# Expert weights in one kernel of a hybrid decoder step: down weights as 8 KB pieces, gate and up products by even and odd columns

## The reference

```python
def swiglu(x, w_g, w_u, w_d):
    return (jax.nn.silu(x @ w_g) * (x @ w_u)) @ w_d

# moe_ffn: each token picks 8 of 64 experts (4 of 8 groups first)
def body(y, inp):
    e, toks, wr = inp
    out = swiglu(x[toks], w_gate[e], w_up[e], w_down[e]) * wr[:, None]
    return y.at[toks].add(out), None
```

## Time and profile before

| what | value |
|---|---|
| time, median of 3 runs | 1742.17 us (1738.51 to 1746.92) |
| the profiled execution's own time | 1733.91 us |
| its span | 1732.1 us |
| TensorE busy (matmul) | 1619.7 us, 94% |
| VectorE, ScalarE, GpSimd busy | 708.6, 441.4, 146.3 us |
| moved by DMA | 552.38 MB, 319 GB/s over the span |

### The profile page before, as it was taken

The page is one execution under the profiler, slowest core; times in us unless marked ns, Lnnn a source line. Parts: engine busy times, 40 slices in busy tenths (PEclk is TensorE's granted clock), DMA queues, the critical chain, the costliest instruction groups (busy, mean ns, idle before and its releaser), DMA issues. The chain is left out here.

```text
span 1732.1 us, 30697 instructions
## 1 busy us (share of the span) xinstructions
PE 1619.7 (94%) x11617; PEld 968.6 (56%) x11744; DVE 708.6 (41%) x1912; ACT 441.4 (25%) x993; POOL 146.3 (8%) x206
## 2 busy tenths in 40 slices
PE   5999898899999999999998998889999999999997
PEld 4677575555555555555466766665555555555554
DVE  3133427263333333333336944165733333333334
ACT  2210113122222222222232124132222222222223
POOL 0000300000000000000020024000000000000000
PEclk9899789899999999999999969999999999999999
DMA  9875534999999999999682533546999999999990
GB/s 364 342 267 177 206 122 165 364 382 402 416 414 417 416 412 413 415 416 412 246 304 74 195 118 116 201 176 271 391 408 417 415 416 415 414 415 416 413 384 27
DMA packets 139032, 552.38 MB, mean 319 GB/s; under 512 B 19407, under 2 KB 36637, under 8 KB 104662
## 3 DMA queue, kind: packets, MB, share of 16 engines
q1 hardware_dynamic: 120562, 513.82, 74.8%
q0 software_dynamic: 15392, 34.66, 5.7%
q10 hardware_dynamic: 3012, 3.00, 0.6%
HBM read 562.74 MB, written 8.60 MB: 330 GB/s over the span
## 5 line engine op out<-in xcount | busy, mean ns | idle before, releaser
L1370 PE MATMUL PS<-ring,arena 128*64 128x256 f32 x4288 | 492.4, 383 | 2.5 <-ACT arena L1689 1.5
L1370 PEld LDWEIGHTS PS<-ring,arena 128*64 128x64 f32 x4288 | 305.1, 138 | 183.5 <-issue 40.0
L1394 PE MATMUL PS<-ring,arena 128*64 128x512 f32 x1072 | 259.6, 605 | 1.4 <-ACT arena L1674 1.4
L1596 DVE TENSOR_TENSOR arena<-arena,PS 128x128 f32<-128x128 f32 x134 | 38.6, 288 | 375.8 <-ACT arena L1672 369.9
L1333 PE MATMUL PS<-arena 128*128 128x512 bf16 x669 | 169.4, 384 | 15.4 <-issue 9.2
L1580 DVE TENSOR_SCALAR arena<-arena 128x512 bf16<-128x512 f32 x130 | 62.8, 483 | 256.5 <-ACT arena L1683 256.5
L1682 ACT COPY arena<-PS 64x512 f32<-64x512 f32 x134 | 77.5, 578 | 302.2 <-PE PS L1394 302.2
L1394 PEld LDWEIGHTS PS<-ring,arena 128*64 128x64 f32 x1072 | 65.0, 136 | 120.4 <-issue 104.1
L1333 PEld LDWEIGHTS PS<-arena 128*128 128x128 bf16 (+1 forms) x796 | 69.6, 99 | 91.9 <-issue 27.7
L1672 ACT ACTIVATE arena<-PS 128x128 f32<-128x128 f32 x134 | 37.2, 278 | 328.1 <-PE PS L1370 328.1
L1324 PEld LDWEIGHTS PS<-cst,arena 128*128 128x128 f32 x552 | 72.0, 194 | 80.2 <-issue 78.3
(11 more groups left out here) (504 smaller groups left out, 1584.3 us busy)
## 6 DMA issues: line engine op xcount, KB each, us to landing
ring<-in_moe_w_gate SPq DMA_DIRECT2D x134, 1024.0 KB, 8.7
ring<-in_moe_w_up SPq DMA_DIRECT2D x134, 1024.0 KB, 11.0
ring<-in_moe_w_down SPq DMA_DIRECT2D x134, 1024.0 KB, 15.4
ring<-in_w_ada SPq DMA_DIRECT2D x32, 1152.0 KB, 10.9
ring<-in_w_ada SPq DMA_DIRECT2D x16, 768.0 KB, 13.8
ring<-in_gla_w_in SPq DMA_DIRECT2D x8, 1152.0 KB, 12.6
ring<-in_dsa_w_in SPq DMA_DIRECT2D x6, 1024.0 KB, 19.2
arena<-in_state_gla POOLq DMA_DIRECT2D x8, 512.0 KB, 5.9
```

Of the source, the lines that this page charges most:

```text
L1370: m = pe.matmul(PS[64 * half:64 * half + 64, 5, 0:256].rearrange("p (g n) -> p g n", g=2), rows[:, k, CAP * b:CAP * b + CAP], gu[:, :, k, ...
L1394: m = pe.matmul(PS[64 * j:64 * j + 64, 7, :], hTt[b][:, kk * CAP:(kk + 1) * CAP], ring[:, s, 2, kk * D + 512 * j:kk * D + 512 * j + 512], ...
```

## The change

Partition p gets the rows 2p and 2p + 1 of an expert's down matrix, which are neighbours, so a partition's share is one piece of 8 KB. The two halves of the hidden columns are then no longer 0 to 127 and 128 to 255, but the even and the odd ones, so that the turned `hm` has entry 2p in its first half and 2p + 1 in its second. The gate and up product takes them by a step of two floats in its streamed operand. The shared expert's weights (`sp_moe`) are not touched.

```diff
--- before.py
+++ after.py
@@ -1136,13 +1136,11 @@
             return [wg.rearrange("(p k) n -> p (k n)", k=KT), wu.rearrange("(p k) n -> p (k n)", k=KT),
-                    wd.rearrange("(k p) n -> p k n", p=P)]
+                    wd.rearrange("(p k) n -> p (k n)", k=2)]
 
         def load_expert(s, e, l, sem):
             for t, src in enumerate(expert_w(l, e)):
                 dst = ring[:, s, t, :]
-                if t == 2:
-                    dst = dst.rearrange("p (k n) -> p k n", k=2)
                 sp.dma_start(dst, src).then_inc(sem, 16)
 
@@ -1368,7 +1366,7 @@
                     m = pe.matmul(PS[64 * half:64 * half + 64, 5, 0:256].rearrange("p (g n) -> p g n", g=2), rows[:, k, CAP * b:CAP * b + CAP],
-                                  gu[:, :, k, half * P:(half + 1) * P], start=(k == 0), stop=(k == KT - 1), skip_group_check=True)
+                                  gu[:, :, k, half:2 * P:2], start=(k == 0), stop=(k == KT - 1), skip_group_check=True)
```

## The result

The changed kernel takes 1762.61 us (median; 1756.98 to 1764.04), the kernel before 1744.55 us. The ratio is 1.0122, 95% interval 1.0097 to 1.0146: slower by about 1.2%, 18 us. The forecast was no change.

The account below looks back on a forecast made before the run. The prediction took TensorE to pace the expert loops, with loads hidden. 1733.9 us profiled + 0 for loads + 0 for the product = 1733.9 us, or 1742 us for the median; range 1726 to 1808 us.

Parts of the forecast that it names:

- TensorE sets the pace: In the two expert loops TensorE was taken as the limit, busy 97.4%, with an expert taking 7.87 us.
- The loads are hidden: Expert weight loads land before use, 3.2 us in hand late in the first loop; cheaper down loads contribute 0 us.
- the creep of the landing time: In the first loop the down load's landing time rises by 2.5 us from the middle to the end.
- The price of a piece: Each DMA packet costs 15 ns beyond its bytes, so larger down pieces save 0.12 us an expert, hidden beside TensorE.
- The sign that was to go with it: In the changed kernel the down load was to land 2.5 us behind the up load, not 5.
- The step of two floats costs 0: In the gate and up product, the streamed operand's step of 8 bytes was taken to add 0 us.
- The reading that led to 0: From L1324's weight loads, 0.83 ns a fetch; two floats a fetch give 0.41 ns a column, as now, cost 0.
- The other reading, from L1977: For the gate and up product, 1.06 ns a fetch gives 0.53 against 0.41 ns a column: 31 ns a pass, 132 us.
- The rule that the prediction cites: SBUF reads keep full bandwidth with two hits per 16-byte line; a step of 8 bytes has two, so 0 us.
- rival B: The strided gate and up stream is slower: a partial price gives 26 to 66 us (1768 to 1808); chance 0.28.
- half-fetch price: In the gate and up product a fetch yields two useful floats, costing 31 ns a pass, 132 us.
- rival C: Loads are the loops' hidden pace, so the change is faster: 1726 us, or at most 1715; chance 0.11.

Follow-up runs that it names:

- short_4k: Kernel before with the gate and up product cut from eight to five contraction slices, down weights in 4 KB pieces: 1724.49 us, ratio 0.9976, with 136 expert bodies.
- short_8k: Kernel before with the same cut to five slices, down weights in 8 KB pieces and neighbouring columns: 1715.68 us, ratio 0.9926, with 136 expert bodies.
- pieces_2k: Kernel before with the down weights as four pieces of 2 KB a partition: 1746.73 us against 1740.15, ratio 1.0037.
- stride_only: Kernel before with only the gate and up product's step of two floats, down weights still in 4 KB pieces: 1760.99 us against 1740.15, ratio 1.0111.
- forms: Kernel before with 19 groups of passes added at its end, read in the profile only: steps of 1, 2, 3, 4 floats take 108, 113, 171, 227 ns a pass.
- other_slice: Changed kernel with the odd half taking contraction slices four ahead, so both streams read different 16-byte lines: 1762.51 us, ratio 1.0127.
- forms2: Kernel before with 13 more groups at its end (pairs, quads, eights, bfloat16), profile only: quads take 3.45 us a group filling lines, 3.64 us across lines.

## Why the prediction was wrong

- **TensorE sets the pace: right.** The edit on TensorE's passes alone gave 1.0111, the whole change 1.0122, the loads alone (in layer 1) 0.9998.
- **The loads are hidden: right, closer than thought.** The kernel before loads an expert in 7.92 us (119.19 MB in 300 us) and uses one in 7.865; the creep of the landing time fits this 0.7%, and the four slots of the ring carry it through 64 experts. The price of a piece was read as 15 ns and measured as 9 (short_4k against short_8k) and as 10 (pieces_2k: 8.06 - 7.895 us over 16 pieces). The term's contribution, 0, holds. The sign that was to go with it, a down load that lands 2.5 us behind the up load, came true (10.3 against 8.3 us), but it tells little: stride_only shows 11.2 against 8.9 us with 4 KB pieces.
- **The step of two floats costs 0: the step that failed.** The prediction laid a price of 0 and one of 31 ns a pass side by side and took 0. It was 5.2 ns. The reading that led to 0 has two faults. It took L1324's weight loads, 0.83 ns for a float on a line of its own, as the price of a line for a streamed operand; the forms show 1.77 ns for that. (0.83 ns need not be the price of a line at all: the loads of ordinary products with neighbours, L2462 and L2503 in forms, take 137 ns for 64 columns and 190 for 128, and that is 0.83 ns a column too.) And it set half of 0.83 against 0.41 ns a column, which is the spacing of two passes at once; one stream takes 0.84 ns a column. Two floats a line take 1.77/2 = 0.885 ns a column, against this 0.84. The other reading, from L1977, had the right form, half a line's price against a column's, but a line there costs 2.1 ns, not 1.77, and since the cost is a small difference of two near numbers, this made 31 ns out of 5. Why a line costs more in L1977 is open; no form had its step of 512 bytes.
- **The rule that the prediction cites.** The Trainium skill ("SBUF — State Buffer", in the note on SBUF cachelines) has lines of 16 bytes and full bandwidth from two hits a line on. The lines are borne out by the quads, aligned and moved. The threshold is not exact here: two float32 a line are 5% short, and in bfloat16 four a line are 5% short and two a line cost a factor of 2.1. The measurement decides.
- **The range held by its rival, not by its forecast.** 1762.6 us lies within 1726 to 1808, which had been drawn wide enough for rival B, with a chance of 0.28. B is what happened, at a sixth of the half-fetch price and so somewhat under its band, which began at 26 us. The reason that it gave first, two halves that share something, was not the cause: two halves on different lines pay the same (other_slice), and so does a full operand, one stream alone (forms).
- **That every nanosecond of a pass is paid 4288 times,** as the prediction said under rival B, was right: 5.2 ns x 4288 = 22 us, the loops grew by 20 (22 against forms), the time by 18 with the whole change and by 21 with the step alone.
- **TensorE's idle 27.5 us** in rival C was in good part missing records, so that rival's room was smaller than stated.

A version that beats both kernels did not come out of this. The 8 KB pieces would pay where TensorE needs less than 7.9 us an expert, and there only if the order of entries costs TensorE nothing.

## What to carry to other kernels

Where TensorE has no slack, look at how many 16-byte lines each streamed operand touches, and not only at the number of columns: in these runs it took 1.69 to 1.80 ns a line, so float32 neighbours have room, a step of two is just over, a step of three takes 1.6 times as long and a step of four twice. Whole aligned lines with gaps between them cost nothing extra. Before a load is made cheaper, ask who waits for it: in a ring, SyncE waiting for a free slot means that the loads are early. And when an ablation breaks the values, count the instructions before reading its time, since values can steer the amount of work.

## What was not expected of the hardware

- The price of a line is per stream: two column halves that stream at once pay it each at the same time (226 ns for 128 lines, both alone and together), whether they read the same lines or others.
- The price of a line stayed at 900 ns for 512 lines when the granted clock fell from 1.00 to 0.50 (forms2), where a pass over neighbours doubles its time.
- Weight loads pay less for a wide step than streams do: a load of 128 floats at 32 bytes takes 193 ns in all, 1.51 ns a float with its fixed part, against 1.80 ns (230 ns x 2 / 256) for the stream at the same step.
- Eight 64 x 64 passes took 0.39 us of TensorE's time in the loop, though they ran two at a time; 0.16 us of it lies between the last start and the next product. Why that gap is as long is open.
